# Weaving the two weight tiles of a pair column by column, in a two-layer hybrid encoder kernel

## The reference

```python
D_MODEL = 1024; SEQ = 512; DEPTH = 2; N_HEADS = 16; D_RNN = 1408; D_FF = 2816
for l in range(DEPTH):
    x = x + 0.5 * swiglu(rms_norm(x, norm_ffn1[l]), ffn1_w_gate[l], ffn1_w_up[l], ffn1_w_down[l])
    h = rms_norm(x, norm_mix[l])
    xr, yr, q, k, v, g_a, g_b = jnp.split(h @ w_in[l], IN_SPLITS, axis=-1)
    hr = rg_lru(causal_depthwise_conv(xr, conv_w[l], conv_b[l]), ...)   # block-diagonal gates, then a scan
    y_a = (jax.nn.gelu(yr) * hr) @ w_up_a[l]
    y_b = chunked_attention(rms_norm(q, q_gain), rms_norm(k, k_gain), v, rel_table[l]) @ w_up_b[l]
    x = x + (sigmoid(g_a) * y_a + sigmoid(g_b) * y_b) @ w_out[l]
    x = x + 0.5 * swiglu(rms_norm(x, norm_ffn2[l]), ffn2_w_gate[l], ffn2_w_up[l], ffn2_w_down[l])
```

## Time and profile before

| | |
|---|---|
| median of 3 runs | 2779.49 us |
| the profiled execution's own time | 2780.0 us |
| its span in the trace | 2778.2 us |
| PE busy | 2734.7 us (98%), 11968 matmuls |
| PEld busy | 2196.4 us (79%), 11968 loads |
| ACT, POOL, DVE busy | 1188.3, 1179.1, 833.2 us |
| DMA | 263.82 MB, mean 95 GB/s |
| mean granted TensorE clock | 0.996 of full speed |

### The profile page before, as it was taken

The page is one execution under the profiler, slowest core; times in us unless marked ns, Lnnn a source line. Parts: engine busy times, 40 slices in busy tenths (PEclk is TensorE's granted clock), DMA queues, the critical chain, the costliest instruction groups (busy, mean ns, idle before and its releaser), DMA issues.

```text
span 2778.2 us, 35532 instructions
## 1 busy us (share of the span) xinstructions
PE 2734.7 (98%) x11968; PEld 2196.4 (79%) x11968; DVE 833.2 (30%) x1515; ACT 1188.3 (43%) x1680; POOL 1179.1 (42%) x524
## 2 busy tenths in 40 slices
PE   7999999999999999999999999999999999999998
PEld 6888878878776688888888888788787757888887
DVE  4222035630015432221132211448100164322212
ACT  5443235742445534443243432457324364444422
POOL 3444444445442234444444444344453423444444
PEclk9999999999999999999999999999999999999999
DMA  7333223332331233332333323332333212333322
GB/s 259 99 91 102 94 85 97 91 100 84 98 98 41 71 91 99 98 98 91 100 99 98 92 91 99 87 93 84 110 96 97 72 40 88 95 91 99 98 92 91
DMA packets 247056, 263.82 MB, mean 95 GB/s; under 512 B 9040, under 2 KB 233072, under 8 KB 246928
## 3 DMA queue, kind: packets, MB, share of 16 engines
q1 hardware_dynamic: 242768, 253.70, 30.6%
q10 hardware_dynamic: 4160, 8.47, 0.9%
HBM read 259.95 MB, written 10.57 MB: 97 GB/s over the span
## 4 chain that ended last, share of the span: by engine, by line
issue 40%; PE 40%; POOL 18%; DVE 1%; POOLq 1%; ACT 0%; DMA 0%; DVEq 0%; ACTq 0%
POOL wlo L414 18%; PE ps L1095 10%; PE ps L1100 10%; PE ps L1099 10%; PE ps L1295 2%; PE ps L1223 2%; PE ps L1277 1%; PE ps L1208 1%; PE ps L1244 1%; PE ps L1239 1%; PE ps L1243 1%; POOLq L421 0%; POOLq L413 0%; PE ps L1325 0%; DVE p L1013 0%
## 5 line engine op out<-in xcount | busy, mean ns | idle before, releaser
L414 POOL TENSOR_TENSOR wlo<-raw,whi 128x1024 fp32r<-128x1024 f32 x475 | 1140.7, 2408 | 1464.1 <-ACT whi L463 1463.7
L1095 PE MATMUL ps<-h_lo,whi 128*128 128x512 f32 x2400 | 945.9, 394 | 21.8 <-DVE h_lo L748 9.8
L1100 PE MATMUL ps<-h_hi,wlo 128*128 128x512 f32 x2400 | 936.5, 390 | 0.0
L1099 PE MATMUL ps<-h_hi,whi 128*128 128x512 f32 x2400 | 936.4, 390 | 0.0
L463 ACT ACTIVATE whi<-raw 128x1024 fp32r<-128x1024 f32 x475 | 500.2, 1056 | 737.3 <-PE ps L1095 676.4
L1095 PEld LDWEIGHTS ps<-h_lo,whi 128*128 128x128 f32 x2400 | 452.0, 188 | 126.9 <-DVE h_lo L748 14.9
L1099 PEld LDWEIGHTS ps<-h_hi,whi 128*128 128x128 f32 x2400 | 452.4, 188 | 96.6 <-issue 3.8
L1100 PEld LDWEIGHTS ps<-h_hi,wlo 128*128 128x128 f32 x2400 | 452.0, 188 | 94.9
L1095 PE MATMUL ps<-act_lo,whi 128*128 128x512 f32 x704 | 273.9, 389 | 0.0
L1099 PE MATMUL ps<-act_hi,whi 128*128 128x512 f32 x704 | 273.9, 389 | 0.0
L1100 PE MATMUL ps<-act_hi,wlo 128*128 128x512 f32 x704 | 273.9, 389 | 0.0
(11 more groups left out here) (139 smaller groups left out, 2635.6 us busy)
## 6 DMA issues: line engine op xcount, KB each, us to landing
raw<-in_w_in SPq DMA_DIRECT2D x124, 512.0 KB, 3.7
raw<-in_w_gate SPq DMA_DIRECT2D x88, 512.0 KB, 3.7
raw<-in_w_up SPq DMA_DIRECT2D x88, 512.0 KB, 3.7
raw<-in_w_down SPq DMA_DIRECT2D x80, 512.0 KB, 3.4
raw<-in_w_up_b SPq DMA_DIRECT2D x19, 512.0 KB, 3.6
rel_band<-rel_rows ACTq DMA_DIRECT2D x1, 8192.0 KB, 39.7
raw<-in_w_out SPq DMA_DIRECT2D x16, 512.0 KB, 3.4
raw<-in_rg_band SPq DMA_DIRECT2D x14, 512.0 KB, 3.5
```

The costliest lines, as they stand in the source:

```text
L414: nc.gpsimd.tensor_tensor(wlo[:, s, :], raw[:, s, :], whi[:, s, :].bitcast(F32), ALU.subtract).then_inc(lo_made, 1)
L1095: ins = pe.matmul(ps[:, b, :], w_hi, x_lo, start=start, stop=False)
L1099: pe.matmul(ps[:, b, :], w_hi, x_hi, start=False, stop=False)
L1100: return pe.matmul(ps[:, b, :], w_lo, x_hi, start=False, stop=stop)
```

## The change

In DRAM, the two 128-column tiles of every pair are woven: columns 0 and 128 of the pair come first, then 1 and 129, and so on. `columns` then takes every second element, from `at + m` on: 128 values, 8 bytes apart, over 1024 bytes of the row. `single` gets its own accessor, `whole`, which reads side by side as before. The parts of `w_in` for `v` and for the eleventh tiles of `xr` and `yr` stay plain. The tiles of `rg_band` are woven two by two, and line 1189 addresses them so. The weaving is a fixed reordering of the arrays before the launch.

```diff
             def columns(s, at, m):
-                return whi[:, s, at + m * P:at + (m + 1) * P], wlo[:, s, at + m * P:at + (m + 1) * P]
+                return whi[:, s, at + m:at + PAIR:2], wlo[:, s, at + m:at + PAIR:2]
+
+            def whole(s, at):
+                return whi[:, s, at:at + P], wlo[:, s, at:at + P]
...
-                    ins = product(b, *columns(s, kk * P, 0), hi[:, kk, :], lo[:, kk, :], kk == 0, kk == KD - 1)
+                    ins = product(b, *whole(s, kk * P), hi[:, kk, :], lo[:, kk, :], kk == 0, kk == KD - 1)
...
-                    ins = product(b, *columns(s, n % BPC * P, 0), u_hi[:, kk, :], u_lo[:, kk, :], first, last)
+                    ins = product(b, *columns(s, n % BPC // 2 * PAIR, n % 2), u_hi[:, kk, :], u_lo[:, kk, :], first, last)
...
+    def woven(w):
+
+        pairs = w.reshape(*w.shape[:-1], -1, 2, P).swapaxes(-2, -1)
+        return np.ascontiguousarray(pairs).reshape(w.shape)
...
+    whole = KR // 2 * PAIR
+    w_in = np.concatenate([a["w_in"][:, :, c:d] if plain else woven(a["w_in"][:, :, c:d]) for c, d, plain in (
+        (XR0, XR0 + whole, False), (XR0 + whole, YR0, True), (YR0, YR0 + whole, False), (YR0 + whole, Q0, True),
+        (Q0, V0, False), (V0, G0, True), (G0, G0 + 2 * D, False))], axis=2)
+    for n in ("ffn1_w_gate", "ffn1_w_up", "ffn1_w_down", "ffn2_w_gate", "ffn2_w_up", "ffn2_w_down", "w_up_a", "w_up_b",
+              "w_out"):
+        a[n] = woven(a[n])
...
-        "w_in": a["w_in"], "rg_band": band, "w_up_a": a["w_up_a"], "w_up_b": a["w_up_b"], "w_out": a["w_out"],
+        "w_in": w_in, "rg_band": woven(band), "w_up_a": a["w_up_a"], "w_up_b": a["w_up_b"], "w_out": a["w_out"],
```

## The result

| | before | after |
|---|---|---|
| runs | 4 | 4 |
| median | 2779.85 us | 2845.13 us |
| lowest to highest | 2779.24 to 2780.95 | 2842.62 to 2846.25 |
| profiled execution | 2780.0 us | 2846.25 us |
| its span | 2778.2 us | 2844.4 us |

The changed kernel is slower: the ratio is 1.0233, with a 95% interval of 1.0215 to 1.0251, that is 65 us. The time lies in the predicted range, between the forecast and rival A (2920 us). The forecast itself, no change, had a chance of 0.48 and did not come true.

What follows compares the result with a forecast made beforehand. The prediction took PE's matmul rate, 0.2267 us per fp32r matmul, as the bound. It summed 2780.0 + 0 + 0 + 0 = 2780.0 us, with a range from 2776 to 2925 us.

Steps and rivals of the forecast that it cites:

- rival A: Every matmul of pair and the bands: toll grows with bytes walked over, 544 to 576 cycles, 140 us, 2920 us; chance 0.32.
- the likeliest case: Whole kernel: no change, 2780.0 us, own range 2778 to 2785 us; chance 0.48 of lying within 0.2%.
- What bounds the kernel: Whole kernel: PE's matmul rate is the limit, 0.2267 us each; a chunk takes 5.44 us against POOL's 2.41 us.
- DMA, ACT, POOL at 0: Chunk preparation: same 1 KB rows and same steps over all 1024 values, cost 0; POOL has 3.0 us of cover.
- The column rate: 10,500 loads with a step of two: at worst half rate, recorded 292 ns instead of 188, still hidden; term 0.
- the cover: Steady stretch: half-rate loads start 214 ns apart, matmuls 227 ns apart, so 13 ns remain and the load is hidden.
- Loads behind waits: Line 1095: 35 loads not started ahead, 104 ns more each at half rate; taken 0, upper end 3.6 us.
- Interference with the moving read: 10,500 matmuls beside stepped loads: taken 0; ends 141 us gained, 2,100 us lost.
- the 13.4 ns: Each fp32r matmul at 2.4 GHz: time beyond the 213.3 ns of its 512 columns, 32 cycles.
- The second reason that I gave for 0: After the f32 sums: period 237 ns with the very same loads, where a strict toll by bytes would give 226.7 ns.
- Rival B: Stepped loads become the bound: 3670 us at a third of the column rate, 4760 us at a quarter; chance 0.08.
- Rival C: Matmuls behind stepped loads: extra is a collision that a stepped load escapes; 2639 us, or 2710 if half gone; chance 0.10.

Runs made afterwards that it cites:

- the ladders: Kernels computing no layer, PE alone running stretches of matmuls, varying load step, starts and column counts; 512 fp32r columns took 226.7 ns at step 1, 233.3 at step 2.

## Why the prediction was right and wrong

The range held; the likeliest case, no change, failed. Slower had a chance of 0.42, but 2845 us is the time of no case: it lies between the forecast and A, and it is luck that a range drawn for A took it in.

**What bounds the kernel.** Right: PE's rate is the limit. The longer period came out almost whole in the time: 68.3 us between starts, 66.2 us of span.

**DMA, ACT, POOL at 0.** Right, shown by the woven data alone: ratio 0.9999.

**The column rate.** The bound was halved at most, recorded 292 ns and hidden. Measured 194 ns, and 118 ns between starts where nothing hides it. The Trainium skill's rule of two accesses in a 16-byte line (SBUF — State Buffer, section "Door 1: The DMA port swizzle") fits: a step of two runs at nearly full rate and a step of four, one value in a line, at half. So the term was 0, but for the second reason and not for the one that the sum used, the cover. The cover was worked out from a halved rate of 110 + 104 = 214 ns between starts, 13 ns less than the period. A load that does run at half the rate starts every 233.3 ns, 6.6 ns more than the period: had a step of two halved the rate, it would not have been hidden, and the time, by this estimate, would have been near 2850 us.

**Loads behind waits, 0 to 3.6 us.** It went the other way: the long intervals shrank by 3.4 us, as PE came later to its waits, and a load is recorded only 5 to 6 ns longer.

**Interference with the moving read, taken as 0.** This is the step that failed: +68.3 us. I had seen that the 13.4 ns vanish at the lower clock and in f32, so that two reads might meet, and then read "the period is 0.2267 us in whichever slot the weights lie" as a sign that addresses don't matter. It is no such sign. Every tile that these loads and moving reads take starts a multiple of 512 bytes into its buffer, and the buffers lie at such distances too: the kernel puts fillers (`line_up`, with `LINE` = 512) in front of them, and their sizes are multiples of 512 bytes. The trace held one relation of addresses only. The Trainium skill says that load and moving read have ports of their own, and that a load takes no bandwidth from a running matmul (TensorE: Matmul & The Clock Gate, section "Step-by-step: what each phase is for"). For fp32r at the upper clock level the runs don't bear this out: shifting either read alone changes the period, from 226.7 up to 236.7 ns.

The second reason that I gave for 0, the wider periods behind the f32 sums, spoke rightly against a strict toll, but not for 0. The kernel before comes back to 226.7 ns ten matmuls later, with the same loads:

```profile
732.49 0.39 PE L1100 MATMUL ps<-h_hi,wlo 128*128 128x512 f32 x1
...
735.21 0.39 PE L1100 MATMUL ps<-h_hi,wlo 128*128 128x512 f32 x1
```

That is twelve matmuls in 2.72 us, while the ten intervals from 730.17 to 732.49 are 225 to 236 ns long. Tiles that lie well still give a longer period for a while, so how the two reads lie to each other in time seems to count beside their addresses; no run varied that by itself.

**Rival A** (a toll by bytes walked over, 2920 us) had the right sign and place and the wrong mechanism. It asked for 576 cycles, and 560 were measured. It then failed with larger steps, with fewer moving columns and with loads of 64.

**Rival B** (the load as the bound) did not occur at a step of two. It does occur at a step of four: 233.3 ns with 256 or 384 moving columns, and nearly all of the 235.1 with 512. B began at more than twice the column time; by this measurement twice is enough.

**Rival C** (a collision that depends on how the two walk) named the mechanism that the ladders bear out for loads side by side, with the wrong sign. With 512 moving columns the kernel before was already in the best of all forms tried, so none of them could gain. My argument against it was the mistaken one above.

What is shown: at the upper clock level, an fp32r matmul of 512 columns behind a load of 128 values side by side costs 544 or 545 cycles if the two reads start a multiple of 256 bytes apart and both at multiples of 32 bytes. In the other relations tried it costs 549 to 568. bf16 is free of it for every load start and step tried, and f32 with 512 columns for every step; the starts were not varied in f32. For the step of two it is shown that the reads make the loss, that the load's own rate doesn't, and that it hangs on the number of moving columns. That it is the same meeting of two reads is inferred: with a step of two, no pair of starts brought 226.7 ns back.

What stays open is the unit in which the two reads meet, why a load of 64 values meets it worse than one of 128, and what the 32 cycles are that remain in the best case. They are 32 with 256, 384, 496 and 512 moving columns (120.0, 173.3, 220.0, 226.7 ns), but 37 to 40 with 432 to 480 and with 504 (196.0 to 216.6, and 226.7 ns), so they are no fixed price of a matmul either.

## What to carry to other kernels

Where fp32r matmuls follow each other at the upper clock, keep weight tiles and moving tiles of 512 columns at starts that are multiples of 32 bytes and differ by multiples of 256, and load whole tiles of 128 values side by side: here a start 8 bytes off cost 52 us of 2780, and a step of two 65 us. A step of two in a load is nearly free by itself (118 ns between starts for 112), so look for its loss in the period between matmuls, not in the load's recorded time; a step of four halves the load's rate (233 ns) and makes it the bound. And a number that is equal everywhere in a trace tells nothing about a quantity that the trace never varies.

## What the runs showed of the hardware that was not expected

A load of 32 or 64 values can make a matmul of 512 columns slower than one of 128: 231.6, 230.0 and 226.7 ns. With 256 moving columns a load's start that is 8 bytes off is faster than an aligned one, 115.6 for 120.0 ns. A moving read with a step of two takes 453 ns for 512 columns, twice 226.7; with a step of four it is 461 ns. Loads at half the rate start 233.3 ns apart, more than twice the 112 ns of the full rate. The loss isn't the sum of single losses: one stepped load in three cost 4.4 ns a matmul, all three 6.7 ns.
